# Squares of a norm added by VectorE and GpSimd ahead of a single ones-matmul per token half

## The reference, cut to what matters

```
def rmsnorm(x, w):
    x32 = x.astype(jnp.float32)
    y = x32 * lax.rsqrt(jnp.mean(x32 * x32, axis=-1, keepdims=True) + NORM_EPS)
    return (y * w.astype(jnp.float32)).astype(x.dtype)
...
for l in range(DEPTH):
    x = x + 0.5 * m[2] * swiglu(modulate(rmsnorm(x, norm_w[l, 0]), m[0], m[1]), ffn1_w13[l], ffn1_w2[l])
    h = modulate(rmsnorm(x, norm_w[l, 1]), m[3], m[4])
    y, yc = mixer(h, hc, w_in[l], ...)
    x = x + m[5] * y
    x = x + 0.5 * m[8] * swiglu(modulate(rmsnorm(x, norm_w[l, 2]), m[6], m[7]), ffn2_w13[l], ffn2_w2[l])
```

## Time and profile before

| | |
|---|---|
| median of three runs | 2220.11 us (2219.54 to 2220.8) |
| the profiled execution's own time | 2220.36 us |
| its span (first to last instruction) | 2218.5 us |
| TensorE busy | 2201.5 us, 99% of the span |
| VectorE busy | 1378.9 us, 62% |
| ScalarE busy | 912.4 us, 41% |
| GpSimd busy | 205.7 us, 9% |
| ones-matmuls of the norms | 43, each in two passes, 86 records of 379 ns (median) |

### The profile page before, as it was taken

The page is one execution under the profiler, slowest core; times in us unless marked ns, Lnnn a source line. Parts: engine busy times, 40 slices in busy tenths (PEclk is TensorE's granted clock), DMA queues, the critical chain, the costliest instruction groups (busy, mean ns, idle before and its releaser), DMA issues.

```text
span 2218.5 us, 29916 instructions
## 1 busy us (share of the span) xinstructions
PE 2201.5 (99%) x12353; PEld 1919.9 (87%) x12353; DVE 1378.9 (62%) x1863; ACT 912.4 (41%) x1368; POOL 205.7 (9%) x313
## 2 busy tenths in 40 slices
PE   8999999999999999999999999999999999999999
PEld 7888888988888888888888898888889899999997
DVE  6988822667566564586763267665227867667754
ACT  4322212557644454342222143222126766555442
POOL 0000000000432340000000000000000033320000
PEclk9999999999999999999999999999999999999999
DMA  9776522221222222356552236565332233336864
GB/s 326 215 231 191 179 96 97 76 75 41 77 76 77 76 77 76 114 154 188 169 154 96 100 112 198 179 189 171 101 100 88 69 124 114 115 129 188 245 185 158
DMA packets 300385, 300.86 MB, mean 136 GB/s; under 512 B 9648, under 2 KB 267288, under 8 KB 300248
## 3 DMA queue, kind: packets, MB, share of 16 engines
q1 hardware_dynamic: 299648, 298.69, 43.6%
q10 hardware_dynamic: 600, 0.25, 0.0%
HBM read 297.86 MB, written 1.05 MB: 135 GB/s over the span
## 4 chain that ended last, share of the span: by engine, by line
PE 91%; DVE 3%; ACT 2%; POOL 2%; DMA 1%; issue 1%; SPq 0%; DVEq 0%; ACTq 0%
PE PS L1909 14%; PE PS L1910 14%; PE PS L1915 14%; PE PS L1895 6%; PE PS L1897 6%; PE PS L1896 6%; PE PS L1929 4%; PE PS L1934 4%; PE PS L1930 4%; PE PS L2459 2%; PE PS L2518 1%; PE PS L2009 1%; PE PS L2470 1%; PE PS L2179 1%; PE PS L2180 1%; PE PS L2181 1%
## 5 line engine op out<-in xcount | busy, mean ns | idle before, releaser
L1191 DVE TENSOR_TENSOR WL<-raw,WH 128x1024 fp32r<-128x1024 f32 x412 | 497.7, 1245 | 343.7 <-ACT WH L718 342.9
L718 ACT CAST WH<-raw 128x1024 fp32r<-128x1024 f32 x412 | 412.5, 1047 | 371.8 <-PE PS L1897 259.5
L1909 PE MATMUL PS<-hH,WH 128*128 128x512 f32 (+1 forms) x1536 | 541.8, 363 | 0.5 <-DVE sg L1456 0.5
L1910 PE MATMUL PS<-hL,WH 128*128 128x512 f32 (+1 forms) x1536 | 538.3, 361 | 0.0
L1915 PE MATMUL PS<-hH,WL 128*128 128x512 f32 (+1 forms) x1536 | 335.3, 361 | 0.0
L1909 PEld LDWEIGHTS PS<-hH,WH 128*128 128x128 f32 x1536 | 290.1, 189 | 44.7 <-DVE sg L1456 0.9
L1910 PEld LDWEIGHTS PS<-hL,WH 128*128 128x128 f32 x1536 | 290.1, 189 | 43.9 <-issue 0.7
L1915 PEld LDWEIGHTS PS<-hH,WL 128*128 128x128 f32 x1536 | 263.9, 189 | 44.2
L1219 DVE SCALAR_TENSOR_TENSOR mraw<-mraw,cst 128x1024 f32<-128x1024 f32 x196 | 242.3, 1280 | 16.2 <-DMA mraw<-in_w_mod 15.3
L1895 PE MATMUL PS<-hidH,WH 128*128 128x512 f32 (+1 forms) x576 | 214.4, 372 | 0.0
L1896 PE MATMUL PS<-hidL,WH 128*128 128x512 f32 (+1 forms) x576 | 213.9, 371 | 0.0
(11 more groups left out here) (277 smaller groups left out, 3503.7 us busy)
## 6 DMA issues: line engine op xcount, KB each, us to landing
raw<-in_ffn_w SPq DMA_DIRECT2D x176, 512.0 KB, 5.2
mraw<-in_w_mod SPq DMA_DIRECT2D x132, 512.0 KB, 4.7
raw<-in_w_in SPq DMA_DIRECT2D x52, 1024.0 KB, 5.3
raw<-in_ffn_w SPq DMA_DIRECT2D x44, 1024.0 KB, 4.9
raw<-in_w_branch_attn SPq DMA_DIRECT2D x8, 1024.0 KB, 5.2
raw<-in_w_branch_gla SPq DMA_DIRECT2D x8, 1024.0 KB, 5.2
raw<-in_w_out SPq DMA_DIRECT2D x8, 1024.0 KB, 5.1
mfirst_b<-in_w_mod SPq DMA_DIRECT2D x8, 512.0 KB, 12.0
```

The lines of the kernel that those rows point to most:

```text
L718: nc.scalar.copy(half(WH, n % 2, e, rows), half(raw, n % 2, e, rows)).then_inc(hi_ready, 1)
L1191: nc.vector.tensor_tensor(half(WL, n % 2, e, rows), half(raw, n % 2, e, rows), half(WH, n % 2, e, rows).bitcast(F32), ALU.subtract).then_i ...
L1909: mm(o, wh[:, kt, cols], rh[:, kt, 0:T], start=kt == 0, stop=False)
L1910: mm(o, wh[:, kt, cols], rl[:, kt, 0:T], start=False, stop=False)
```

## The change

All eight tiles of squares are now added into `sq[:, 0]` before the ones-matmul, which runs over that one tile.

- Norm 0, half 1: GpSimd adds all seven further tiles (`add_first_squares`, first in its queue). Half 0 keeps its eight matmuls.
- Norms 1 to 5: tiles 6 and 7 are added by VectorE in a new `add_last_squares`, for both halves. In half 0 it stands right behind the last `residual` of that half; in half 1 behind that half's last residual and ahead of the low parts of the second weight unit's column part 1. A new semaphore `sq_all` counts these adds. Tile 7's add waits for tile 6's, and in half 1 of norms 1, 3 and 4 tile 6's waits for GpSimd's last add.
- `sums` waits for `sq_all` and issues one matmul.
- In norm 2 `sums(2, 0)` moves two feature tiles later in the output projection; in norm 5 it moves behind the eight transposes of the first token tile.

In numbers: 25 ones-matmuls fewer on TensorE (7 in norm 0, two in each of the nine sums of norms 1 to 5), 18 adds more on VectorE, 7 more on GpSimd.

```diff
         def adds_c(n):
-            return (ADDED - 1) * (n - n // 3)
+            return KT - 1 + (ADDED - 1) * (n - n // 3)
+
+        def all_at(n, c):
+            return (KT - ADDED) * (2 * (n - 1) + c + 1)
...
+            def add_first_squares():
+                for kt in range(1, KT):
+                    pool.wait_ge(sq_done, half_at(0, kt, 1))
+                    if kt > 1:
+                        pool.wait_ge(sq_add_c, kt - 1)
+                    nc.gpsimd.tensor_tensor(sq[:, 0, S:T2], sq[:, 0, S:T2], sq[:, kt, S:T2], ALU.add).then_inc(sq_add_c, 1)
...
                     for kt in range(WAIT_C[n] + 1, KT):
                         residual(n, kt, 1)
+                    for kt in range(ADDED, KT):
+                        add_last_squares(n, 1, kt)
                     prep(second, only=1)
...
+            def add_last_squares(n, c, kt):
+                own, at = slice(c * S, (c + 1) * S), all_at(n, c) - KT + kt
+                dve.wait_ge(sq_done, half_at(n, kt, c))
+                if kt > ADDED:
+                    dve.wait_ge(sq_all, at)
+                elif c and FULL[n] == 0:
+                    dve.wait_ge(sq_add_c, adds_c(n))
+                else:
+                    dve.wait_ge(sq_add, (ADDED - 1) * n)
+                nc.vector.tensor_tensor(sq[:, 0, own], sq[:, 0, own], sq[:, kt, own], ALU.add).then_inc(sq_all, 1)
...
                     elif kt <= ADDED:
                         add_squares(m, kt - 1, 0)
+                for kt in range(ADDED, KT):
+                    add_last_squares(m, 0, kt)
                 for kt in range(WAIT_C[m]):
                     residual(m, kt, 1)
...
                 residual(m, KT - 1, 0)
+                for kt in range(ADDED, KT):
+                    add_last_squares(m, 0, kt)
...
-                for kt in tiles or few:
-                    if n and kt == 0 and c and FULL[n] == 0:
-                        pe.wait_ge(sq_add_c, adds_c(n))
-                    elif n and kt == 0:
-                        pe.wait_ge(sq_add, (ADDED - 1) * n)
...
+                    if n:
+                        pe.wait_ge(sq_all, all_at(n, c))
                     else:
-                        pe.wait_ge(sq_done, half_at(n, kt, c))
-                    ins = mm(PS[:, sum_bank(n, c), own], ones[:], sq[:, kt, own], start=kt == first, stop=kt == last)
-                if kt == last:
-                    ins.then_inc(ss_done, 1)
+                        pe.wait_ge(sq_add_c, KT - 1)
+                    ins = mm(PS[:, sum_bank(n, c), own], ones[:], sq[:, 0, own], start=True, stop=True)
+                ins.then_inc(ss_done, 1)
...
-                    sums(3 * l + 2, 0)
+                    pe.wait_ge(x_ready, half_at(3 * l + 2, KT - 1, 0))
                     for tok in range(S // P):
+                        if tok:
+                            sums(3 * l + 2, 0)
...
-                            if c and m == 0 and kt == KT // 2:
+                            if c and m == 0 and kt == KT - 2:
                                 sums(3 * l + 2, 0)
```

More of the change, by code:

```diff
@@ L250, in hybrid_backbone @@
         sq_add_c = sem("sq_add_c")
+        sq_all = sem("sq_all")
         ss_done = sem("ss_done")
@@ L663, in add_squares @@
                     pool.wait_ge(sq_done, half_at(n, kt, 1))
-                    if n > 1 or kt > 1:
-                        pool.wait_ge(sq_add_c, adds_c(n) - ADDED + kt)
+                    pool.wait_ge(sq_add_c, adds_c(n) - ADDED + kt)
                     nc.gpsimd.tensor_tensor(sq[:, 0, S:T2], sq[:, 0, S:T2], sq[:, kt, S:T2], ALU.add).then_inc(sq_add_c, 1)
@@ L678, in sinks @@
                                             ALU.add).then_inc(at_den, 1)
+            add_first_squares()
             for l in range(DEPTH):
@@ L2113, in _, with sums @@
                     ins.then_inc(x_t, 1)
-            def sums(n, c, tiles=None):
+            def sums(n, c):
                 own = slice(c * S, (c + 1) * S)
@@ L2119, in sums @@
                     pe.wait_ge(x_ready, half_at(n, sum_bank(n, c), norm_tokens(n) // S - 1))
-                few = (KT - 2, KT - 1, 0) if c else (0, KT - 2, KT - 1)
-                first, last = (0, KT - 1) if tiles else (few[0], few[-1])
-                for kt in tiles or few:
-                    if n and kt == 0 and c and FULL[n] == 0:
-                        pe.wait_ge(sq_add_c, adds_c(n))
-                    elif n and kt == 0:
-                        pe.wait_ge(sq_add, (ADDED - 1) * n)
-                    else:
-                        pe.wait_ge(sq_done, half_at(n, kt, c))
-                    ins = mm(PS[:, sum_bank(n, c), own], ones[:], sq[:, kt, own], start=kt == first, stop=kt == last)
-                if kt == last:
-                    ins.then_inc(ss_done, 1)
+                if n == c == 0:
+                    for kt in range(KT):
+                        pe.wait_ge(sq_done, half_at(n, kt, c))
+                        ins = mm(PS[:, sum_bank(n, c), own], ones[:], sq[:, kt, own], start=kt == 0, stop=kt == KT - 1)
+                else:
+                    if n:
+                        pe.wait_ge(sq_all, all_at(n, c))
+                    else:
+                        pe.wait_ge(sq_add_c, KT - 1)
+                    ins = mm(PS[:, sum_bank(n, c), own], ones[:], sq[:, 0, own], start=True, stop=True)
+                ins.then_inc(ss_done, 1)
             pe.wait_ge(ones_in, 16)
             pe.wait_ge(x_ready, KT + 1)
-            sums(0, 0, range(KT))
+            sums(0, 0)
             pe.wait_ge(x_ready, 2 * KT)
@@ L2144, in _ @@
             pe.wait_ge(vec_ready, 1)
-            sums(0, 1, range(1))
             first_turn(0)
-            sums(0, 1, range(1, 2))
-            sums(0, 1, range(2, KT))
+            sums(0, 1)
             def ffn(k):
```

## The result

The changed kernel takes 2228.8 us (median of five executions, 2225.62 to 2231.42) against 2220.31 us before (five, 2219.54 to 2220.8): ratio 1.0036, 95% interval 1.0025 to 1.0047, so 8.5 us slower. The direction was that of the forecast (+4.1 us); the size was twice as large, and the median lies above the range (2221.5 to 2226.5).

What follows compares the result with a forecast made beforehand. TensorE, though 99% busy, was taken to be paced by ScalarE's and VectorE's chain at the norms. Terms 5.4 - 1.7 + 0.45 + 0 = +4.1 us gave 2224.2 us, range 2221.5 to 2226.5.

Steps and rivals of the forecast that it cites:

- What bounds the kernel: Around the norms: TensorE, though 99% busy, is paced by the chain of log, exp, `scaled` and `hH` on ScalarE and VectorE.
- a tile 0.43 us: Ones-matmul on TensorE: one tile, two passes, takes 0.43 us; all 25 removed tiles, if won, give 10.8 us.
- Norms 1, 3, 4, half 0: Tile 7's add delays half 1's residuals and squares, so log and first weight unit come 0.8 us late per norm.
- Half 1: Norms 1, 3, 4: VectorE's two serial adds behind GpSimd's last add cost 1.0 us beyond half 0's delay, 1.8 together.
- The low part of the weights: VectorE, half 1 of norms 1, 3, 4: it moves behind the adds but stays hidden with 1.4 us to spare.
- the term +5.4: Norms 1, 3, 4: sum and chain of half 1 move 1.8 us each, +5.4 us for three, bounds 4.8 to 6.6.
- the sinking clock: Sign against the prediction: TensorE's granted clock sinks after the new waits; no size or chance given.
- Norm 0: Before the first projection: removing seven tiles only lengthens TensorE's wait for ScalarE's cast, 0 us, bounds -0.3 and +0.3.
- rival (d): Norm 0: GpSimd's add chain ends at 29.9, some 5.5 us past the need, giving 2229.7 us; chance 0.03.
- a first call costs about 6 us more: Norm 0: by this rule GpSimd's adds would end at 24.3, the whole about 0.2 us later.
- Norm 2: Both halves: neither sum waits, and each wins two tiles, -1.7 us together, bounds -0.9 to -1.7.
- norm 5: Half 0 only: tile 7's add delays the sum from 2022.60 to 2023.06, +0.45 us, bounds 0.4 to 0.6.

Runs made afterwards that it cites:

- e5_norm0: The kernel before with norm 0 alone changed (GpSimd's seven adds, one ones-matmul in place of eight): +0.9 us, its interval taking in zero.
- e10_fill_all: The changed kernel with filler products ahead of half 1's sum in norms 1, 3, 4 and seven filler ones-matmuls in norm 0: 2225.10 us, ratio 1.0020.
- e1_fill: The changed kernel with 12 filler products ahead of half 1's sum in norms 1, 3 and 4, norm 0 not filled: 2225.97 us, ratio 1.0024.
- e4_norm2: The kernel before with norm 2 alone changed: 1.4 us faster than before.
- the split: The kernel before with norm 2 changed and, in half 1 of norms 1, 3, 4, GpSimd and VectorE adding separate tiles, two ones-matmuls: 2218.7 us.
- e2_half1: The kernel before with half 1 of norms 1, 3 and 4 alone changed: 2226.7 us, +6.2 us.
- e8_half1_fill: The kernel before with only half 1 of norms 1, 3, 4 changed, plus 12 filler products ahead of each of these sums: 2223.57 us, ratio 1.0013.

## Why the prediction was wrong

- **What bounds the kernel; a tile 0.43 us.** Right. No removed tile was won outside norm 2.
- **Norms 1, 3, 4, half 0, +0.8 each.** Right: 0.78 in norm 1 by the log, +2.7 for three (forecast 2.4). The granted clock stayed at 1.00 behind these waits of 0.7 to 1.0 us in every profile.
- **Half 1, +1.0 each.** The wait is right: GpSimd's last add, 0.11 us to wake (0.05 in the sum), 0.95 us for two adds, 1.80 us of idle TensorE; with the clock kept up 1.05, 1.06 and 1.00 us. The low part of the weights stayed hidden, as said.
- **The step that failed** is the conversion of that wait into time: "the chain for half 1 moves by the same 1.8", and with it the term +5.4. It took TensorE to go on behind the wait at its old speed. After a stop of 1.8 us it goes on at 1.2 GHz for about 3.5 us in many cases, and its work there then takes longer than the chain: each of the three norms cost 3.3 to 3.7 us in the profiled execution. The prediction named the sinking clock among what would make it wrong, and gave it neither a price nor a chance. Between the medians with and without filling at all four places lie 8.5 - 4.6 = 3.9 us, nearly half of the result.
- **Norm 0, 0.** Wrong by the same omission. The prediction saw "an idle TensorE of about 2 us before the first projection" and priced it at 0, with a bound of +0.3. It costs 0.9 us (e5_norm0, e10_fill_all against e1_fill, and the profiles with a fall against those without). GpSimd's seven adds there took 5.96 us from 12.27 and ended at 18.23, ahead of the sum at 21.75, so rival (d) is out. The prediction also weighed the rule of the Trainium skill, GPSIMD Engine Reference, section 2.1 Instruction dispatch, by which a first call costs about 6 us more. The runs can't tell: in after a record `MODIFY_POOL_CONFIG` of these adds' line stands at 1.1 us, and GpSimd then sat idle for 11.11 us until ScalarE's squares came, in which such a load could hide.
- **Norm 2, -1.7; norm 5, +0.45.** Right: -1.74 in the ledger of e10_fill_all and -1.4 by e4_norm2; 0.5 by the rows.
- **The rest of 4.6 against 4.1** is 0.3 to 0.4 in norm 3, which costs that much more than norm 4 in each of the three profiles with the full change: VectorE's two dependent adds stand 0.88 us apart there instead of some 0.5, in after:

```profile
1316.91 0.42 DVE L1453 TENSOR_TENSOR sq<-sq 128x256 f32<-128x256 f32 x1 [1.27 <-POOL sq L678]
1317.79 0.42 DVE L1453 TENSOR_TENSOR sq<-sq 128x256 f32<-128x256 f32 x1 [0.46 <-DVE sq L1453]
```

## What to carry to other kernels

An idle TensorE has two prices: the wait itself, and the slower work behind it. Where a change stops TensorE for as long as here (1.8 us) amid busy work, or thins its work out as in norm 0, price the products that follow at half the clock, even where the idle time itself is hidden, and give the case a chance rather than a mention. If such a wait can't be avoided, cheap products into a place that is overwritten anyway win back the second price; better is to distribute the work so that no engine's last step waits for another's, as the split did: one ones-matmul more in half 1, and 6.6 us less.

## What the runs showed that was not expected

- Waits of 1.79, 1.80 and 1.81 us in one execution of e2_half1 had one fall of the clock between them; those of 1.80, 2.15 and 1.81 us in the changed kernel's had three. The mean clock of each execution was the sign of it, and the spread of the times: 5.2 us in e2_half1, 1.5 with the filling, 0.6 for ten of eleven in e10_fill_all.
- A fall is short and dear: about 3.5 us at 0.50, 0.7 to 1.5 us lost in a norm of the profiled executions.
- The gap between two dependent VectorE adds was 0.88 us from start to start in norm 3 in three kernels with the full change, and about 0.5 in norms 1 and 4 of the same executions and in all three norms of e8_half1_fill. The runs do not say why.
